# Prompt attention of a hybrid encoder layer: the order of a pair's logits units on TensorE, the first loads of a stage, and who issues the last row stores

## What is computed

```
p  = softmax(q_a . k - slope * dist, masked)              # 8 A heads, 64 wide
oA = p @ v_a
p0, p1 = softmax of the two maps of a B head
oB = rmsnorm((p0 - lambda * p1) @ v_b) * gain             # 4 B heads, 128 wide
h  = x + [oA, oB] @ w_o
y  = rmsnorm(h + relu(rmsnorm(h) @ w_up)^2 @ w_down)
```

## Time and profile before

| what | value |
|---|---|
| median of 3 runs | 3878.54 us (3877.07 to 3885.38) |
| profiled execution, device time | 3880.51 us |
| its span, first to last instruction | 3878.7 us |
| PE busy in the span | 3504.6 us (90%) |
| stage p, about | 977 to 1321 us |
| stage f, about | 1325 to 2191 us |
| stage r, about | 2197 to 2922 us |
| stage g, about | 2926 to 3879 us |

### The profile page before, as it was taken

One profiled execution on the slowest core, in us unless ns is written; L12 is line 12 of the kernel. 1 busy time (PEld: TensorE's weight loads), 2 busy tenths in 40 slices (PEclk: granted clock), 3 DMA queues, 4 the chain that ended last, 5 costly groups with the idle time before them and its releaser, 6 DMA issues. The chain is left out here.

```text
span 3878.7 us, 49946 instructions
## 1 busy us (share of the span) xinstructions
PE 3504.6 (90%) x19049; PEld 2953.6 (76%) x19049; DVE 2142.1 (55%) x3853; ACT 1867.5 (48%) x2907; POOL 254.8 (7%) x442
## 2 busy tenths in 40 slices
PE   8998997776799689998999699999996999999997
PEld 6886786334588578887888488888885888799996
DVE  4334764887466367777776555555553434443333
ACT  2213443664366367786776255565552333332331
POOL 1000010000010110002000100001001000100000
PEclk9998998887799899999999799999998999999998
DMA  5547445541831322433432441111104323322221
GB/s 156 156 139 233 148 151 186 191 154 25 209 77 43 132 87 87 143 116 120 143 108 96 142 140 36 48 38 42 35 6 142 109 98 109 131 81 72 87 70 45
DMA packets 231295, 419.86 MB, mean 108 GB/s; under 512 B 28832, under 2 KB 129184, under 8 KB 221856
## 3 DMA queue, kind: packets, MB, share of 16 engines
q1 hardware_dynamic: 189808, 333.93, 26.8%
q0 software_dynamic: 17072, 71.68, 5.6%
q10 hardware_dynamic: 24192, 11.24, 1.1%
HBM read 336.69 MB, written 80.12 MB: 107 GB/s over the span
## 5 line engine op out<-in xcount | busy, mean ns | idle before, releaser
L1293 PE MATMUL rPV<-rV,rPTr 128*128 128x64 f32 (+1 forms) x2592 | 337.6, 271 | 0.7 <-ACT rPTr L1361 0.7
L1293 PEld LDWEIGHTS rPV<-rV,rPTr 128*128 128x128 f32 x2592 | 326.2, 191 | 10.8 <-issue 1.1
L2478 ACT ACTIVATE gRU<-gUP 128x512 f32<-128x512 f32 (+1 forms) x64 | 41.8, 653 | 497.7 <-PE gUP L2318 497.7
L1361 ACT ACTIVATE rPTr<-rTP 128x512 f32<-128x512 f32 (+1 forms) x360 | 189.2, 553 | 164.2 <-PE rTP L1282 161.6
L1345 ACT ACTIVATE rX<-rX,rmx 128x1168 f32<-128x1168 f32 (+7 forms) x128 | 210.7, 1646 | 116.2 <-DVE rmx L1423 115.9
L2318 PE MATMUL gUP<-gA_hi,gW_hi 128*128 128x320 f32 (+2 forms) x784 | 222.9, 334 | 7.8 <-DVE gW_lo L2520 6.1
L2318 PE MATMUL gUP<-gA_hi,gW_lo 128*128 128x320 f32 (+2 forms) x784 | 222.6, 334 | 0.0
L2318 PE MATMUL gUP<-gA_lo,gW_hi 128*128 128x320 f32 (+2 forms) x784 | 222.5, 334 | 0.0
L2318 PE MATMUL fUP<-fA_hi,fW_hi 128*128 128x512 f32 (+1 forms) x544 | 208.0, 382 | 15.2 <-DVE fW_lo L2520 11.2
L951 ACT ACTIVATE fajunk<-faS,fav 128x2064 int8<-128x2064 f32 (+4 forms) x120 | 205.6, 1714 | 12.1 <-DMA y<-fY 9.8
L2520 DVE TENSOR_TENSOR fW_lo<-fW_raw,fW_hi 128x2048 fp32r<-128x2048 f32 x72 | 163.4, 2291 | 81.4 <-ACT fW_hi L2420 81.4
(11 more groups left out here) (408 smaller groups left out, 8761.2 us busy)
## 6 DMA issues: line engine op xcount, KB each, us to landing
fW_raw<-w_up SPq DMA_DIRECT2D x32, 1024.0 KB, 5.1
fW_raw<-w_down SPq DMA_DIRECT2D x32, 1024.0 KB, 5.0
gW_raw<-w_up SPq DMA_DIRECT2D x32, 1024.0 KB, 5.0
gW_raw<-w_down SPq DMA_DIRECT2D x32, 1024.0 KB, 4.9
qT<-qOUT SPq DMA_DIRECT2D x40, 512.0 KB, 3.3
sKB<-cache_kb SPq DMA_DIRECT2D x8, 2048.0 KB, 13.5
sVB<-cache_vb SPq DMA_DIRECT2D x8, 2048.0 KB, 8.1
kT<-ktz ACTq DMA_DIRECT2D x17, 640.0 KB, 4.1
```

The source lines that it names most:

```text
L1293: mm = pe.matmul(pv[:, 0:size], PTr[n % 3][:, j - 4 * k, :], V[:, j, a:a + size], start=(j == 0), stop=(j == blk[t] - 1))
L1361: act.activation(PTr[n % 3][:, 0:size, :], TP[bank_use[("p", n)] % 2][:, 0:size, :], ACT.Copy).then_inc(s_pt, 1)
L2478: act.activation(RU[:, 0:nt * P].rearrange("p (n w) -> p n w", n=n), UP[f % 2][:, 0:n, 0:width], ACT.Relu).then_inc(s_ru, 1)
```

## The change

In the prompt attention a B pair's `apply` (odd m) now issues all units of jobs g + 2 and g + 3, unit u between T(u+1) and Pu as far as there are groups, the rest ahead of the last product; the even job of a pair issues none. Orders of A jobs stay. The first query block and the slice of DT that the first tile needs are loaded ahead of the rest, the latter on a semaphore of its own, and DVE and ACT do lambda after jobs 0 and 1. The last index-score units end a step earlier. In the feed-forward ACT issues the first two loads of TR and the order of splitting is o, w, o, w, ...; in the last group of tiles SP, not POOL, issues the row stores.

```diff
 def units_of(s):
-    return mine[len(mine) * max(bi - 1, 0) // (QBLK - 1):len(mine) * bi // (QBLK - 1)]
+    steps = QBLK - 1 if gi < NGR - 1 else QBLK - 2
+    return mine[len(mine) * max(bi - 1, 0) // steps:len(mine) * min(bi, steps) // steps]
...
-            queries(QA, 0, 0, H_A, s_qa)
-            keys(0)
-            for dst, src in ((DT[:, :], dist), (idn[:, :], ident), (lam4, lambdas), (gB[:, :], sub_g)):
+            first, rest = (slice(0, 1), slice(1, ABLK))
+            for part, done in ((first, s_q0), (rest, s_qa[0])):
+                for copy in range(2):
+                    sp.dma_start(QA[0][copy * DH:(copy + 1) * DH, :, :, :].bitcast(F32)
+                                 .rearrange("d (h b) u q -> d h b (u q)", h=2)[:, :, part, :],
+                                 qT[T0, :, part, :, :].rearrange("(h d) b u q -> d h b (u q)", h=2)).then_inc(done, 16)
+                if part == first:
+                    keys(0)
+                    sp.dma_start(DT[:, nearest[0]:PKEYS], dist[:, nearest[0]:PKEYS]).then_inc(s_d0, 16)
+            for dst, src in ((idn[:, :], ident), (DT[:, 0:nearest[0]], dist[:, 0:nearest[0]]), (lam4, lambdas),
+                             (gB[:, :], sub_g)):
...
-                early = g + AHEAD < NG and groups[t] > 1
+                G = groups[t]
+                ahead = [j for j in ((g + AHEAD,) if m < H_A else (g + AHEAD - 1, g + AHEAD)) if j < NG]
+                units = [(j, k) for j in ahead for k in range(halves[j // JOBS])]
+
+                def logits_between(i):
+                    for u, (j, k) in enumerate(units):
+                        at = u if m > H_A else 0 if u == 0 and G > 1 else G - 1
+                        if i == min(at, G - 1):
+                            logits(j, slice(k, k + 1))
+
                 transposes(0)
-                for k in range(1, groups[t]):
+                for k in range(1, G):
                     transposes(k)
-                    if k == 1 and early:
-                        logits(g + AHEAD, slice(0, 1))
+                    logits_between(k - 1)
                     products(k - 1)
-                if g + AHEAD < NG:
-                    logits(g + AHEAD, slice(1, None) if early else slice(None))
-                products(groups[t] - 1)
+                logits_between(G - 1)
+                products(G - 1)
...
                 if applied(g):
                     apply(g)
-                elif g + AHEAD < NG:
-                    logits(g + AHEAD)
...
# feed_forward, SP, last group of tiles
+                else:
+                    for t in range(nt):
+                        sp.wait_ge(s_t5, g * NT1 + t + 1)
+                        sp.dma_start(y[token(g, t):token(g, t) + P, :], Y[:, t, :]).then_inc(s_ye, 16)
+                    sp.wait_ge(s_ye, 16 * nt)
# POOL
-            load_o(0, 0)
-            load_o(0, 1)
...
-                    pool.wait_ge(s_t5, g * NT1 + t + 1)
-                    pool.dma_start(y[token(g, t):token(g, t) + P, :], Y[:, t, :]).then_inc(s_y, 16)
                     if not final:
+                        pool.wait_ge(s_t5, g * NT1 + t + 1)
+                        pool.dma_start(y[token(g, t):token(g, t) + P, :], Y[:, t, :]).then_inc(s_y, 16)
# ACT
+            for t in range(2):
+                act.dma_start(TR[t][:, :, :], oT[:, :, token(0, t):token(0, t) + P]).then_inc(s_o0[t], 16)
+            o_hi_part(0, 0)
             for j in range(4):
                 w_hi_part(0, 0, j)
-                o_hi_part(0, j)
+                if j < 3:
+                    o_hi_part(0, j + 1)
```

More of the change, by code:

```diff
@@ L1084, in attend_prompt @@
         s_d0 = sem("s_d0")
+        s_q0 = sem("s_q0")
+        s_first = sem("s_first")
         s_x0 = sem("s_x0")
@@ L1222, in _ @@
             pool.wait_ge(s_c, 64)
+            pool.wait_ge(s_d0, 16)
             if first_masked > 0:
@@ L1246, in logits @@
                 t, m = divmod(g, JOBS)
+                if g == 0:
+                    pe.wait_ge(s_q0, 32)
                 if m == 0:
                     pe.wait_ge(s_ka[t], 16)
+                if m == (1 if t == 0 else 0):
                     pe.wait_ge(s_qa[t % QR], QDMA * (t // QR + 1))
@@ L1388, in _ @@
                 dve.memset(X[i][:, :], 0.0).then_inc(s_x0, 1)
[L1390 to L1400, removed]
             dve.wait_ge(s_x0, XB)
@@ L1480, in finish_scale @@
                 ins.then_inc(s_fo, 1)
+            dve.wait_ge(s_d0, 16)
             if first_masked == 0:
@@ L1484, in _ @@
                 dve.scalar_tensor_tensor(DA[0][:, 0:n_of[0]], DA[0][:, 0:n_of[0]], -BIG,
-                                         DT[:, nearest[0]:PKEYS], ALU.mult, ALU.add).then_inc(s_d0, 1)
-                dve.wait_ge(s_d0, 1)
+                                         DT[:, nearest[0]:PKEYS], ALU.mult, ALU.add).then_inc(s_first, 1)
+                dve.wait_ge(s_first, 1)
             take(0)
             take(1)
+            dve.wait_ge(s_c, 64)
+            for i in range(2):
+                dve.tensor_tensor_reduce(out=OM[:, i * DH:(i + 1) * DH], in0=lam4[:, 2 * i, :],
+                                         in1=lam4[:, 2 * i + 1, :], scale=1.0, scalar=0.0,
+                                         op0=ALU.mult, op1=ALU.add, accum_out=lv[:, i:i + 1]).then_inc(s_lam, 1)
+            dve.wait_ge(s_lam, 3)
+            dve.tensor_tensor(lv[:, 4:5], lv[:, 3:4], lv[:, 2:3], ALU.subtract).then_inc(s_lam, 1)
+            dve.wait_ge(s_lam, 4)
+            dve.tensor_scalar(lv[:, 5:6], lv[:, 4:5], -LAM_INIT, None, ALU.add).then_inc(s_lam, 1)
+            dve.tensor_scalar(gB[:, :], gB[:, :], 1.0 - LAM_INIT, None, ALU.mult).then_inc(s_lam, 1)
+            dve.wait_ge(s_lam, 6)
             for g in range(NG):
@@ L2110, in feed_forward @@
         s_o = [sem(f"s_o{i}") for i in range(2)]
+        s_o0 = [sem(f"s_o0{i}") for i in range(2)]
         s_ohi = sem("s_ohi")
@@ L2131, in feed_forward @@
         s_y = sem("s_y")
+        s_ye = sem("s_ye")
         def chain(name, tiles, rows):
@@ L2424, in o_hi_part @@
                 tok = slice(t * P, t * P + P)
-                act.wait_ge(s_o[t % 2], g * (NT1 * 8) + 16 * (t // 2 + 1))
+                if g == 0 and t < 2:
+                    act.wait_ge(s_o0[t], 16)
+                else:
+                    act.wait_ge(s_o[t % 2], g * (NT1 * 8) + 16 * (t // 2))
                 act.activation(A_hi[:, :, tok], TR[t % 2][:, :, :], ACT.Copy).then_inc(s_ohi, 1)
+            for t in range(2):
+                act.dma_start(TR[t][:, :, :], oT[:, :, token(0, t):token(0, t) + P]).then_inc(s_o0[t], 16)
             if hosted:
                 act.dma_start(bd[:, 1:PT], bounds[:, 1:PT]).then_inc(s_bd, 16)
+            o_hi_part(0, 0)
             for j in range(4):
                 w_hi_part(0, 0, j)
-                o_hi_part(0, j)
+                if j < 3:
+                    o_hi_part(0, j + 1)
             def group(g, nt, final):
@@ L2530, in o_lo_part @@
                 a_lo_part(s_ohi, g * NT1 + t + 1, t, s_olo)
+            o_lo_part(0, 0)
             for j in range(4):
                 w_lo_part(0, 0, j)
-                o_lo_part(0, j)
+                if j < 3:
+                    o_lo_part(0, j + 1)
             dve.wait_ge(s_c, 48)
```

6 lines of the change are left out of this document (3 added, 3 removed).

## The result

| what | before | after |
|---|---|---|
| median of 4 runs | 3880.65 us | 4012.52 us |
| ratio, 95% interval | | 1.034 (1.032 to 1.036) |
| span of the profiled execution | 3878.7 us | 4009.1 us |
| stage q's end (start of s) | 640.96 | 637.53 |
| stage s, start to next start | 336.61 | 338.62 |

A forecast was written before the change was run, and what follows sets the result against it. TensorE was taken to bound the whole kernel, but a loop of waits the prompt attention's B pairs. Terms +79 +32 +10 -7 -2.5 -1.2 -2.3 -5 -6.6 made +96.4, forecasting 3975 us; own bounds 3945 to 4005, range 3920 to 4022.

The forecast's parts named there:

- The B order with three and four groups: Stage r: odd job's last unit waits behind ACT's copy; 3.55 us per pair in tile 14, 1.4 in tile 8; +79 in all.
- The way to the next tile: Stage r, last combine to next tile's first: one pair's lengthening again, 17.3 us over tiles 8 to 14.
- Stage p: Prompt tiles 0 to 7: a unit pushed behind another unit and products, 1.74 us an interval in tiles 3 to 6; +32.
- The clock: Stage r: new PE waits lower the granted clock in a quarter of 35 pairs, 1.1 us each; +10, bounds 0 and 38.
- The starts: Earlier loads and lambda later: r -7, p 0; index-score units a step earlier: q -2.3; feed-forward f -2.5, g -1.2.
- The feed-forward's start: Stages f and g: two loads moved from POOL's queue to ACT's shorten PE's wait; -2.5 and -1.2, worst +1 each.
- The ends: Stages f and g: SP's stores spare POOL's store issue before each next tile; -5 and -6.6, together between -5 and -15.
- The sum: All terms together +96.4 us on the profiled execution's 3880.5, so 3976.9; 3975 for the median.
- the loop isn't lengthened: Rival: copy ready early enough, so the unit isn't held and PE fills its waits; 3802 to 3854 us, chance 0.05.
- only r pays: Rival: slack or the exponent hides the late unit in stage p, so only r gets slower; 3946 us, chance 0.12.
- The clock falls in every pair: Rival: every pair of tiles 7 to 15 has a dip, +38 in place of +10; 4003 to 4010 us, chance 0.15.
- a third unit: Upper bound in stage r: third and fourth units also pushed behind the second copy, another 1 us per pair, +32.

The follow-up runs named there:

- run 3: Changed kernel, but in tiles 7 to 15 both units of job g + 2 stand ahead of the pair's first products; 3924.36 us.
- run 4: Changed kernel, but in B pairs of tiles with three or more groups ACT copies groups 0 and 1 ahead of the even job's exponent; 3929.87 us.
- run 2: Kernel before with only TensorE's B order of the changed kernel put in; 4031.81 us.
- run 5: Changed kernel, but in tiles 3 to 6 (two groups) both units stand ahead of the pair's first products; 3996.37 us.
- Run 6: Changed kernel plus eight extra products per B pair that keep PE busy ahead of its wait for ACT's copy, output unchanged; 4033.52 us.
- run 8: As run 7, but ACT issues the feed-forward's first two loads of TR, splitting order still w, o; 3866.16 us.
- run 9: As run 7, but the feed-forward's splitting order is o, w, with POOL still issuing all loads of TR; 3861.9 us.
- run 1: Changed kernel with TensorE's B order put back to that of before, the rest of the change kept; 3876.36 us, 0.9984 of before.
- run 7: Kernel before plus earlier index-score units, early loads of p and r with lambda later, and SP's stores; feed-forward start as before; 3863.48 us, 0.9946.
- run 10: As run 7, but in tiles 7 to 14 both units of g + 2 precede the pair's first products and ACT copies first; 3855.36 us, 0.9929.

## Why the prediction was right, point by point

**The B order with three and four groups: right, by its mechanism and in size.** Tile 14 was to get 3.55 us longer and got 3.41, tile 8 1.4 and got 1.33; from copy to take 3.30 was reckoned and 3.16 came (the prediction's own rows give 3.51 for tile 14, 2784.0 less 2780.49, and not 3.55). Undoing the wait from PE's side (run 3) and from ACT's (run 4) gives the loss back. Three intervals a tile of the shortest kind make 63.8 us in r, 62.1 with tile 11 at 11.46; the prediction had 62 for them.

**The way to the next tile: as much as one interval, but for the clock.** 17.3 us were put for seven tiles; it is 25.3, near 4.7 in tiles 11 to 14. From tile 10 on the way has a granted clock of 0.97 or 0.98 where it had 1.00 before. Runs 2 and 5, with the same order, have some of these ways at 1.00: 62.28, 65.81, 70.11 and 80.18 us for tiles 11 to 14, so 13.5 us over before in these four, where some 12 were forecast and 18.8 came. The windows of the way from tile 11 to 12, in the changed kernel and in run 2, have the same 460 matmuls in them, and the granted clock tells them apart (third number from the end):

```profile
2583.74:2647.61 63.87, 59.85 (x460) 55.95 (x461) 27.98 (x68) 35.08 (x58) 7.58 (x5) 0.97 0.20 50
```

```profile
2600.50:2662.78 62.28, 58.26 (x460) 54.44 (x461) 28.03 (x69) 35.09 (x58) 7.59 (x5) 1.00 0.20 52
```

**Stage p: 42 us where 32 was forecast.** The interval of tile 6 grew by 1.73 against 1.74, tile 0's by 0.46 against 0.5. The difference is in the last interval of tiles 3, 4 and 6, which grew by 3.2 to 3.3 us, in one of tile 5 (3.0), and in the way from tiles 3, 4 and 6 to the next, 2.5 to 2.7 against 0.77. Here too it is mostly the clock: the four intervals have 0.75 to 0.81, the three ways 0.94 to 0.96. Run 2, with the same order, has the last interval of tile 6 at 1.00, and it is 7.19 us, 1.72 over before; its ways behind tiles 4 and 6, at 1.00, are 1.0 and 1.7 over before. The windows of two intervals of tile 4, as changed:

```profile
1159.48:1165.08 5.60, 3.71 (x26) 3.30 (x26) 3.21 (x9) 2.75 (x7) 0.00 (x0) 1.00 0.00 0
1165.08:1172.39 7.31, 5.22 (x26) 4.70 (x26) 3.34 (x8) 2.73 (x7) 0.00 (x0) 0.77 0.41 91
```

**The clock: the term that was mis-sized most.** +10 was taken, for r alone. In r the intervals over the shortest of their tile make 12.6 us more than in the kernel before, and the ways and stage p have their share, as shown. A rough estimate of the whole is the length of a stage times what its granted clock lacks of 1.00: in r 19.5 us before (0.973) and 41.5 after (0.950), in p 25.2 (0.927) and 35.4 (0.909), so some 32 us more in the two. For r this is clear of the spread: in the profiles with the old order it is 15.5 to 22.5, with the new one (changed kernel, runs 2 and 5) 39.9 to 49.8. In p the clock at the stage's start spreads about as much (last section). Run 6, which brings r to 17.4 by this estimate, takes 17.5 us off r. A dip costs 0.9 to 1.6 us here over the shortest interval of its tile, where the earlier trace rows had 1.1. But the clock does not fall in each pair, as the full term of 38 us would have it: of r's 24 intervals 11 have a granted clock below 1.00, and tiles 8 and 10 and two of three pairs in tile 14 stand at their shortest. The page of the Trainium skill named in the prediction is borne out as to the mechanism, and only in part as to "each time".

**The starts.** Stage r: -7 forecast, -6.8 measured (first combine 64.93 us behind the stage's start, then 58.14). Here DVE's first take comes 13.65 us behind the start, where it was 22.3, and lambda follows behind two jobs; of those 8.7 us 1.9 are lost again:

```profile
2236.07 0.10 POOL L1206 MEMSET rhalf<- 128x4 f32 x1 [5.07 <-POOLq L72]
...
2249.72 1.22 DVE L1432 CUSTOM_DVE_ANT_0 rX<-rLG,rDA 128x1024 f32<-128x1024 f32 x1
...
2255.57 2.41 DVE L1501 CUSTOM_DVE_ANT_0 rOM<-rOT 128x64 f32<-128x64 f32 x1
```

Stage p: -1.3, 0.3 outside its bounds of -1 to +1.5. Stage q: -3.4 where -2.3 was taken and -3 was the bound; the last eviction is out at 632.7, before it began at 635.47. These are single profiles, and the others spread. With the new start of r, eleven profiles have its first combine at 56.9 to 61.6 us behind the start, and the two with the old one at 64.9 and 65.4: that gain is clear. The first combine of p is at 31.3 to 33.7 us against 32.2 and 33.4, and q ends at 636.4 to 640.4 us against 638.9 and 641.0: gains of 1.3 and 3.4 us can't be told from this spread.

**The feed-forward's start: wrong, and beyond its bounds.** -2.5 and -1.2 were forecast, +1 the worst; from start to last product it cost +6.1 in f (850.07, then 856.21) and +6.0 in g. The step that failed is "two loads move from POOL's queue to ACT's": they were taken as the same loads, issued sooner. They are issued 1.4 us sooner and land 5.9 us later, and now ACT and DVE split nothing before they land:

```profile
1379.99 1.06 ACT L2455 ACTIVATE fA_hi<-fTR 128x1024 fp32r<-128x1024 f32 x1 [20.23 <-DMA fTR<-oT]
1380.95 1.89 ACT L2446 ACTIVATE fW_hi<-fW_raw 128x2048 fp32r<-128x2048 f32 x1
```

```profile
1330.46 1.91 ACT L2420 ACTIVATE fW_hi<-fW_raw 128x2048 fp32r<-128x2048 f32 x1 [10.13 <-DMA fW_raw<-w_o]
...
1334.68 1.06 ACT L2426 ACTIVATE fA_hi<-fTR 128x1024 fp32r<-128x1024 f32 x1 [2.31 <-DMA fTR<-oT]
```

The first fence is of after (f starts at 1364.39), the second of before (1324.93): 15.6 us to the part of TR, against 9.75, at which time before had the first weights split as well. Besides, the row that the term was read from the earlier trace rows is PE's second wait in f. That one did end sooner, 33.7 us behind the start and not 34.5; what grew is the first, which the term left out, from 12.2 us to 20.9 in f and from 11.6 to 21.4 in g. Runs 8 and 9 put the late first product down to the queue, and f's loss to the queue and the order together.

**The ends: right in kind, undersized.** From the start of the last product to the next stage 22.7 us became 15.5 in f (-7.2; -5 forecast), and in g 23.82 to the span's end became 14.76 (-9.06; -6.6 forecast). Together that is 16.2, over the bound of 15. The last store stands 11.1 us behind the start of the last product, where it was 17.3. All runs with SP's stores have the same two ends within 0.1 us. The three tiny instructions of POOL follow each other without a store between.

**The sum:** 96.4 us was forecast for the profiled execution and 130.4 came. Of the 34 us, p has 10, r's way to the next tile 8 and r's intervals beyond the clock's +10 4, and these 22 are about what the estimate above gives the clock beyond its term; the feed-forward's start has 16; the ends, q and p's start came out 7 better; s, which the change does not touch, differs by 2.0. The rival "the loop isn't lengthened" fell with run 1, "only r pays" with p's +41. "The clock falls in every pair" was half right in its mechanism, and the result lies above its 4003 to 4010. So the order's mechanism and its price in the intervals were right; that the total still lies in the range of 3920 to 4022 is in part luck, since its upper end was made of the clock and a third unit, and the feed-forward's 16 us were in no case.

## What to carry to other kernels

On an engine that works in order, a unit put behind an instruction that waits takes over that wait, whatever it waits for itself: before moving work "into a gap", look for what ends the gap and ask whether that depends on work which the moved unit feeds. Waits that a trace shows on a busy engine (52 us here) may lie beside the loop that sets the pace; count what the loop's own steps wait for. A new wait on TensorE can cost more than its own length, since the granted clock can fall with it: here some 30 us of 136 in p and r, by estimate. And the parts of a change are better timed by themselves: here three of them together earn 0.5% (run 7), one costs 0.3% (run 1 against 7), and one costs 3.8% (run 2).

## What the runs showed of the hardware

The same four loads of 512 KB went in other packets when ACT issued them. The page's queues of run 7 (POOL issues) and of run 1 (ACT issues; columns: packets, MB, share of 16 engines' span):

```profile
q0 software_dynamic: 15776, 66.96, 5.3%
q10 hardware_dynamic: 24192, 11.24, 1.1%
```

```profile
q0 software_dynamic: 15200, 64.86, 5.1%
q10 hardware_dynamic: 28352, 13.34, 1.5%
```

2.10 MB leave q0 with 576 packets (3.6 KB each) and come to q10 with 4160 (0.5 KB each). While four pieces of w_o and 2 MB of x stand in the other queues, the loads in small packets land later. The Trainium skill ("DMA: Bandwidth & Descriptors", Queues, rings and completion order) says that each engine goes round its queues packet by packet. If the packets that the profile counts are the ones meant, a queue of small packets gets the smaller share by that, which agrees with 15.6 against 9.75 us. No run here varied the size of the packets alone, and a rival stands beside it: on POOL's queue the first two loads of TR were issued ahead of the four of x, and on ACT's queue they run beside them. No run tells the two apart.

The clock at the start of stage p differs between executions: in 10 us of the stretch between tile 0's last combine and tile 1's first (run 7's window ends 0.4 us behind it), run 7 was granted 1.00 (2.4 GHz) and run 10 0.50 (1.2 GHz), by the windows of the two:

```profile
1024.00:1034.00 10.00, 7.75 (x60) 6.59 (x59) 4.83 (x20) 5.46 (x17) 0.00 (x0) 1.00 1.04 223
```

```profile
1025.00:1035.00 10.00, 9.34 (x42) 8.46 (x43) 2.81 (x14) 3.10 (x11) 0.00 (x0) 0.50 1.01 226
```

From tile 0's last combine to tile 1's first it takes 19.7 us in the one and 24.8 in the other. The part of the program is the same; run 1 had it at 25.05 too. Over all thirteen profiles the mean granted clock of this stretch goes from 0.50 to 0.99 and its length from 26.7 to 19.6 us, and both the kernel before and the changed one have it near 20.4. So 5 us of p, more or less, are no matter of the order, and a profile of one execution can show either.
